# A three-block layer kernel: softmax in two steps, one 64-deep product in the delta rule's inversion, bias vectors made between the stages

## The chip, the cores and the metric

The kernel runs on one core of a Trainium2 chip. The metric is device time in microseconds (us) of one execution. Three runs of the kernel before gave 3664.62, 3666.99 and 3671.49 us; the median, 3666.99, is the time that the prediction starts from.

## The reference, cut to what matters

Three different blocks follow each other, on a sequence of 512 tokens (528 in the first, with 16 meta tokens ahead), width 1024:

```python
x = first_block(x, ...)    # RWKV-7 beside differential attention, then an MLP
x = second_block(x, ...)   # gated delta rule, GLA and HGRN2 mixers, then a grouped mixture of experts
x = third_block(x, ...)    # forgetting, block-sparse, stick-breaking and sliding-window attention
```

The change touches one piece of each. In block 1, the differential attention of 8 heads: each head has two softmaxes over the same keys, and its weights are their difference.

```python
s = jnp.where(pos[None, :] <= qpos[:, None], q @ k^T, neg)
pr = jax.nn.softmax(s, axis=-1)
attn_w = pr[:, :, 0] - lam * pr[:, :, 1]
o = attn_w @ v
```

In block 2, the gated delta rule of 4 heads, in chunks of 128 tokens, which solves a unit lower triangular system for each chunk:

```python
t_mat = a_strict + jnp.eye(c)
sol = lax.linalg.triangular_solve(t_mat, rhs, left_side=True, lower=True, unit_diagonal=True)
```

In block 3, two of the four kinds of attention (8 heads in all) add a bias that depends on the distance between query and key alone, looked up in a table of 32 buckets:

```python
s = s + rel_bias_h[:, rel_bucket(dist)]      # NEG_INF where dist < 0
```

## The kernel before

The program is one basic block for each engine, written by Python generators. `K.P`, `K.V`, `K.A` and `K.G` are TensorE (PE), VectorE (DVE), ScalarE (ACT) and GpSimd (POOL), and each records its instructions through helpers of one line each; these lines are the only ones that the profile can name: `tt` L361 (two tensors), `ts` L365 (scalars), `stt` L370, `cp` L373 (copy), `ms` L376 (memset), `rec` L379 (reciprocal), `red` L382, `scan` L385, `act` L346 and `copy` L354 on ScalarE, `mm` L425 and `tr` L429 (transpose) on PE. `did` or a last argument names an event that other engines wait for with `wait_ge(*at(...))`. `P.bank` takes a PSUM bank and waits until it was emptied. Weights stream from memory into a ring of five slabs ("ring"), are rounded by VectorE, ScalarE or POOL (`pool_half` does half a slab) and used by PE; everything else lies in one long SBUF tile ("arena").

The order on each engine is that of the generators. A `yield` ends a step; the next stream then gives its next step. Nothing is reordered: an engine that stands at a wait holds all that is behind it.

**Block 1, heads stage.** Eight pairs of RWKV heads are worked through, while a second stream, the differential attention, is advanced beside them at a pace of 0.7 (`Engine.advance`). In `dve_diff`, `scores(hd, i)` does VectorE's part of tile i of head hd: five query tiles a head (16 rows, then four times 128), their keys 16, 144, 272, 400 and 528 wide; 40 tiles in all. It waits for the scores in PSUM and takes two negated maxima. ScalarE then computes two exponentials with their sums. VectorE waits for each (`df_exp`), inverts the sums, scales the second matrix (`V.ts`) and combines both (`V.stt`). PE transposes these weights for the product with the values. `scores` has no yield of its own; the loop over tiles yields three times behind it (twice for i = 0).

**Block 2, mixers.** `both(delta, linear, 6, gates())` runs the delta rule's streams beside those of the other two mixers on each engine. The inversion of a 128-row triangle works on four chunks at a time, first with diagonal blocks of 32, doubled from 2 to 32 rows by the products Y, Z and ZT for l = 2, 4, 8, 16, then to 64 and 128. In the step Y 64, each chunk takes two products: one 64 rows deep with the second half of the leading triangle (`U.M0`, filled by ScalarE from `U.Xp` and from PE's `gd_m0`), one 32 rows deep with `U.Xp[32:64]`. At l = 2 to 16 VectorE also fills `U.M0` and `U.M1` with masks in turn.

**Block 2, experts' end.** After the last expert product `down(g)` the results go by VectorE and ScalarE copies into `m.ysb`, by DMA into `yd` in memory, and POOL gathers them back for each token into `m.yt` (`e_got`). VectorE adds the residual (L370) and takes the sums for the layer norm, ScalarE and VectorE normalize, and PE transposes (L429) into the layout of block 3.

**Block 3, start.** PE does the forget gate's projection, the first query projection and the root of the norm, then `rounds([dense(), local(), tables()])`: one step of each stream in turn. `dense` and `local` are the projections and attentions; `tables` makes the eight bias vectors. For vector i, VectorE first writes the column of bucket values, broadcast to 32 x 128, into `m.rb`; PE multiplies it with a one-hot matrix of buckets (a pass of high and low parts, so two PE instructions); VectorE copies the product into `m.vec[i % 2]`, whose rest it has set to -1e30; POOL (`pool_block3`) stores it into `skew[i]` in memory (the store is L3995) and loads it back with a row pitch one shorter (L4000), so that each row is shifted by one against the row above. That is `m.table[i]`, which PE adds to the scores of the later tiles. VectorE's rounds hold `forget()` beside these, the forget gate's chain: four ScalarE steps, then five on VectorE, the last a running sum, for which the scaling of the first query waits.

```python
def rounds(streams):
    while streams:
        for s in list(streams):
            try:
                next(s)
            except StopIteration:
                streams.remove(s)
```

Of the kernel before, what the change touches and what calls it, by code (L numbers as in the profile page):

```python
# [1619 lines left out]
def dve_diff(K, m):  # L1620
    V, at, ps, c, p, T, d, lam = K.V, K.book.at, K.ps, K.c, K.p, T1, m.df, m.lam

    def scores(hd, i):
# [25 lines left out]
    for hd in range(8):  # L1649
# [14 lines left out]
        for i in range(5):  # L1664
            scores(hd, i)
            yield
# [315 lines left out]
def memory2(K, x):  # L1982
# [12 lines left out]
    U.ATp, U.Xp, U.XTp, U.M0, U.M1, U.Yp = [M(128) for _ in range(6)]  # L1995
# [29 lines left out]
    m.yt = [m.xs[:, 1024 * j:1024 * j + 1024] for j in range(4)]  # L2025
# [53 lines left out]
def pe_mixers(K, m):  # L2079
# [81 lines left out]
    def delta():  # L2161
        for hd in range(4):
# [214 lines left out]
def act_mixers(K, m, bg):  # L2377
# [44 lines left out]
    def delta():  # L2422
        for hd in range(4):
# [185 lines left out]
def dve_mixers(K, m):  # L2609
# [47 lines left out]
    def delta():  # L2657
        for hd in range(4):
# [63 lines left out]
            for i, l in enumerate((2, 4, 8, 16)):  # L2722
# [8 lines left out]
                V.tt(U.XTp, U.XTp, bk("gd_xt", l, hd)[:, 0:128], ADD, "gd_xt", l, hd)  # L2731
                yield
# [275 lines left out]
def pe_experts(K, m):  # L3008
# [98 lines left out]
    for g in range(GROUPS):  # L3107
# [11 lines left out]
        down(g)  # L3119
    b = [P.bank(1, "normed", "ln2", k) for k in range(8)]  # L3120
# [9 lines left out]
def act_experts(K, m, yd):  # L3130
# [21 lines left out]
    for g in range(GROUPS):  # L3152
# [23 lines left out]
        for s in range(2):  # L3176
# [3 lines left out]
            A.eng.dma_start(yd[r0:r0 + 128, :], m.ysb[s]).then_inc(*K.book.up("yst%d" % s, ("e_st", g, s), by=16))  # L3180
    for j in range(4):
# [8 lines left out]
def dve_experts(K, m):  # L3190
# [27 lines left out]
    for g in range(GROUPS):  # L3218
# [26 lines left out]
        for kk in range(8):  # L3245
            dve_next(K, m.we, i)
            i += 1
        V.wait_ge(*at("slab", "experts", i - 1))
        if g:
            V.wait_ge(*at("e_st", g - 1, 1))  # L3250
        for h in range(2):
            V.cp(m.ysb[1][:, 512 * h:512 * h + 512], out_of(K, 1, T, "e_y", g, 2 + h), "e_y", g, 2 + h)
    for j in range(4):
# [168 lines left out]
def memory3(K, x):  # L3422
# [4 lines left out]
    m.vec, m.rb, m.table = [M(640) for _ in range(2)], M(128), [M(512 if i < 4 else 256) for i in range(8)]  # L3427
    m.d = []
# [36 lines left out]
                next(s)  # L3465
            except StopIteration:
                streams.remove(s)


def pe_block3(K, m):  # L3470
# [41 lines left out]
    def softmax_pair(t):  # L3512
# [4 lines left out]
        def scores(i):  # L3517
# [12 lines left out]
            else:  # L3530
                for r in range(2):
                    n, wide = (hd + r, 512) if kind == "moba" else (4 + hd + r, 256)
                    P.wait_ge(*at("table%d" % (n % 2), n))
# [97 lines left out]
    def tables():  # L3631
        for i in range(8):
            P.wait_ge(*at("tb_rb", i))
# [546 lines left out]
```

## Time and profile before

| | |
|---|---|
| median of three runs | 3666.99 us |
| the profiled execution, its time | 3679.07 us |
| its span in the trace | 3677.2 us |
| granted clock of PE, mean | 0.903 of full |
| busy: PE, DVE, ACT, POOL | 3218.3 (88%), 1663.1 (45%), 1220.4 (33%), 831.4 (23%) us |
| instructions on PE | 30118 |
| read from memory, written | 236.27 MB, 20.05 MB |

The profile was taken on an execution that ran 12 us longer than the median, so each duration below belongs to one of 3679 us. Busy shares are means over stages with different limits: the heads stage lies between 100 and 1126 us, the mixers between about 1780 and 2640, the experts end at 3126, block 3 begins at 3178. PE is the busiest engine everywhere; what an edit is worth depends on whether PE waits at its place, and for whom. A name such as "PE psum L425 <- DVE arena L361" reads: PE, before writing PSUM at line 425, waited for VectorE's operation of line 361 on the arena. In the timeline, what stands in square brackets is the idle time ahead of the instruction and what ended it.

### The profile page before, as it was taken

To read this page: it belongs to the slowest core of one execution; us is meant where nothing else is said; L and a number is where in the kernel's file an instruction comes from. 1 tells how busy PE (TensorE), PEld (TensorE's weight loads), DVE (VectorE), ACT (ScalarE), POOL (GpSimd) and SP (SyncE) were. 2 spreads that over 40 slices of the span, in tenths; PEclk is the share of its full clock that TensorE was granted. 3 is DMA by queue.
4 is the path that set the end of the run, shared out by engine and by line. 5 is a ranking of instruction groups with operands and counts; after the bars stand their busy time and mean duration, and the time that the engine had idled before them with its cause. 6 is when DMAs were issued, how large, how long until landed. Compare 5 with 4: busy or idle time off the path is not lost.

```text
span 3677.2 us, 70665 instructions
## 1 busy us (share of the span) xinstructions
PE 3218.3 (88%) x30118; PEld 2716.8 (74%) x30118; DVE 1663.1 (45%) x2925; ACT 1220.4 (33%) x2079; POOL 831.4 (23%) x808
## 2 busy tenths in 40 slices
PE   7888888898888999999889787887979999688887
PEld 6767777787777999999667666665769998345555
DVE  3544544444432434242343444556656665432342
ACT  2323323322322234232333334433344433232231
POOL 4122121121102200000245353543000002423232
PEclk9888888798877999999999898988999999778998
DMA  3001011010003332232122121213325555211111
GB/s 122 25 28 33 26 34 33 19 40 27 25 20 129 92 110 87 87 92 83 43 59 67 41 61 46 72 56 126 97 58 172 172 160 178 94 35 46 38 46 58
DMA packets 93962, 260.88 MB, mean 71 GB/s; under 512 B 10672, under 2 KB 10672, under 8 KB 92240
## 3 DMA queue, kind: packets, MB, share of 16 engines
q1 hardware_dynamic: 81072, 209.17, 19.2%
q0 software_dynamic: 7680, 35.66, 2.8%
q10 hardware_dynamic: 4896, 11.54, 0.8%
q8 instruction: 237, 3.88, 0.4%
q14 instruction: 77, 0.63, 0.1%
HBM read 236.27 MB, written 20.05 MB: 70 GB/s over the span
## 4 chain that ended last, share of the span: by engine, by line
PE 72%; DVE 13%; ACT 9%; issue 4%; DMA 2%; POOL 0%; DVEq 0%; ACTq 0%; SPq 0%; POOLq 0%
PE psum L425 70%; DVE arena L361 6%; ACT arena L346 5%; DVE arena L370 3%; ACT arena L354 2%; PE psum L429 1%; DMA ring<-in_w 1%; DVE arena L365 1%; ACT L342 1%; ACT L346 1%; DVE arena L382 1%; DVE arena L373 0%; DVE arena L388 0%; DVE arena L385 0%; DMA arena<-in_x 0%
## 5 line engine op out<-in xcount | busy, mean ns | idle before, releaser
L425 PE MATMUL psum<-arena,ring 128*128 128x264 f32 (+3 forms) x7720 | 1669.4, 340 | 24.5 <-DVE arena L361 11.8
L425 PEld LDWEIGHTS psum<-arena,ring 128*128 128x128 f32 (+1 forms) x7720 | 1269.5, 196 | 187.6 <-issue 43.5
L425 PE MATMUL psum<-arena 32*32 32x32 f32 (+19 forms) x16100 | 1027.2, 247 | 332.0 <-DVE arena L361 73.2
L425 PEld LDWEIGHTS psum<-arena 32*32 32x32 f32 (+13 forms) x16100 | 735.1, 138 | 589.6 <-issue 243.6
L425 PE MATMUL psum<-arena,arena 128*128 128x264 f32 (+2 forms) x5440 | 1005.4, 300 | 33.9 <-DVE arena L361 13.0
L425 PEld LDWEIGHTS psum<-arena,arena 128*128 128x128 f32 x5440 | 799.6, 188 | 86.7 <-issue 32.4
L354 ACT ACTIVATE arena<-psum 128x512 f32<-128x512 f32 (+14 forms) x656 | 299.9, 457 | 858.6 <-PE psum L425 703.2
L373 POOL CAST ring<-ring 128x512 fp32r<-128x512 f32 x332 | 221.2, 666 | 1320.8 <-DMA ring<-in_w 1312.1
L361 DVE TENSOR_TENSOR arena<-arena 128x528 f32<-128x528 f32 (+9 forms) x674 | 379.0, 562 | 238.0 <-ACT arena L346 126.9
L361 DVE TENSOR_TENSOR ring<-ring,arena 128x1024 fp32r<-128x1024 f32 (+1 forms) x250 | 293.6, 1174 | 349.4 <-ACT arena L354 346.8
L361 POOL TENSOR_TENSOR ring<-ring,ring 128x512 fp32r<-128x512 f32 x332 | 444.3, 1338 | 26.7
L346 ACT ACTIVATE arena<-arena 128x512 f32<-128x512 f32 (+8 forms) x494 | 292.5, 592 | 392.1 <-DVE arena L361 213.3
L354 ACT ACTIVATE arena<-ring 128x1024 fp32r<-128x1024 f32 (+1 forms) x250 | 254.9, 1020 | 481.3 <-PE psum L425 425.5
L361 DVE TENSOR_TENSOR arena<-arena,psum 88x192 f32<-88x192 f32 (+6 forms) x436 | 177.6, 407 | 406.6 <-PE psum L425 392.8
L370 DVE SCALAR_TENSOR_TENSOR arena<-arena 128x512 f32<-128x512 f32 (+8 forms) x237 | 178.6, 754 | 258.5 <-ACT arena L346 243.6
L346 ACT ACTIVATE arena<-psum,arena 128x528 f32<-128x528 f32 (+8 forms) x206 | 117.1, 568 | 292.4 <-DVE arena L382 180.8
L429 PE MATMUL psum<-arena 128*128 128x128 f32 (+2 forms) x693 | 114.9, 304 | 60.9 <-DVE arena L365 17.7
L429 PEld LDWEIGHTS psum<-arena 128*128 128x128 f32 (+2 forms) x693 | 86.3, 147 | 81.3 <-ACT arena L346 24.6
L361 DVE TENSOR_TENSOR arena<-psum,arena 88x264 f32<-88x264 f32 (+3 forms) x165 | 83.2, 504 | 119.1 <-PE psum L425 57.0
L370 DVE SCALAR_TENSOR_TENSOR arena<-psum,arena 128x528 f32<-128x528 f32 (+2 forms) x89 | 56.7, 638 | 160.8 <-PE psum L425 142.5
L382 DVE TENSOR_REDUCE arena<-psum 128x1 f32<-128x256 f32 (+8 forms) x128 | 57.1, 446 | 125.2 <-PE psum L425 122.2
L365 DVE TENSOR_SCALAR arena<-arena 128x512 f32<-128x512 f32 (+12 forms) x171 | 81.0, 474 | 72.2 <-ACT arena L354 48.8
(47 smaller groups left out, 885.3 us busy)
## 6 DMA issues: line engine op xcount, KB each, us to landing
ring<-in_w SPq DMA_DIRECT2D x202, 512.0 KB, 3.5
ring<-in_w SPq DMA_DIRECT2D x356, 256.0 KB, 2.6
bg<-arena ACTq DMA_DIRECT2D x24, 256.0 KB, 2.1
yd<-arena ACTq DMA_DIRECT2D x10, 512.0 KB, 5.0
arena<-in_x SPq DMA_DIRECT2D x2, 2112.0 KB, 11.3
arena<-bg POOLq DMA_DIRECT2D x1, 3072.0 KB, 18.1
od<-arena POOLq DMA_DIRECT2D x8, 264.0 KB, 3.7
oy<-arena POOLq DMA_DIRECT2D x8, 264.0 KB, 2.3
```

Source lines behind the costliest of these rows:

```text
L342: self.eng.preload_act_table_set("natural_log_exp_and_others")
L346: self.own(self.eng.activation(out, a, f, bias=bias, scale=scale, accum_out=accum), event)
L354: self.own(self.eng.activation(out, a, ACT.Copy, scale=scale), event)
L361: self.own(self.eng.tensor_tensor(out, a, b, op), event)
L365: self.own(self.eng.tensor_scalar(out, a, s1, None, op0), event)
L370: self.own(self.eng.scalar_tensor_tensor(out=out, in0=a, scalar=s, in1=b, op0=op0, op1=op1), event)
L373: self.own(self.eng.tensor_copy(out, a), event)
L382: self.own(self.eng.tensor_reduce(out, a, AXX, op, negate=neg), event)
L425: self.last_ins = self.eng.matmul(out, l, r, start=start, stop=stop, skip_group_check=skip)
L429: self.last_ins = self.eng.transpose(out, a, self.ident[0:n, 0:n])
```

## The change

Three edits, one in each block.

A. `scores` of `dve_diff` becomes a generator and yields once between the two maxima and the wait for the first exponential; one of the yields behind it goes, so that the number of steps stays.

B. The leading 64-row triangle of each chunk is kept in one place, `U.lead`, over the memory of `U.M0` and `U.M1`. Y 64 is one product for each chunk, 64 rows deep and 64 columns wide. ScalarE fills the two diagonal blocks from `U.Xp` (one copy more) and the block below the diagonal from `gd_m0`; VectorE zeroes the block above, behind its last addition for l = 16, and ScalarE's copy from `gd_m0` waits for that (`gd_lead`).

C. The eight bias vectors are made after the experts' last product. PE (`pe_tables`) reads the bucket values as a broadcast column, without `m.rb`; ScalarE copies the odd ones (`act_tables`), VectorE the even ones (`dve_tables`), each behind its last copy of the experts' results; VectorE sets the parts without a bias (`dve_no_tables`) before it waits for the last slab. `m.vec` is eight buffers, in memory that block 3 uses later for its heads (`m.d`), and `m.yt` moves elsewhere. POOL, at block 3's start, rounds four halves of slabs, issues all eight stores, then for each vector a half, the wait for its store, and the load. VectorE waits for all eight stores before its rounds, which have no `tables()` any more.

```diff
@@ dve_diff, scores @@
             V.red(sc[sub][:, 0:1], ps[0:qw, m0:m0 + W], MAX, "df_max", hd, i, sub, neg=True)
+        yield
         V.wait_ge(*at("df_exp", hd, i, 0))
...
         for i in range(5):
-            scores(hd, i)
-            yield
+            yield from scores(hd, i)
             if i:
                 yield
             yield
...
-    U.ATp, U.Xp, U.XTp, U.M0, U.M1, U.Yp = [M(128) for _ in range(6)]
+    U.ATp, U.Xp, U.XTp, U.Yp, U.M0, U.M1 = [M(128) for _ in range(6)]
+    U.lead = M.arena[:, M.top - 256:M.top].rearrange("p (j t) -> p j t", t=64)
...
             for j in range(4):
-                P.mm(bk(b)[64:128, 64 * j:64 * j + 32], U.AT[0:64, 128 * j + 64:128 * j + 128], U.M0[0:64, I4[j]])
-                P.mm(bk(b)[64:128, 64 * j + 32:64 * j + 64], U.AT[32:64, 128 * j + 64:128 * j + 128], U.Xp[32:64, I4[j]])
+                P.mm(bk(b)[64:128, 64 * j:64 * j + 64], U.AT[0:64, 128 * j + 64:128 * j + 128], U.lead[0:64, j, :])
             P.did("gd_inv", "Y", 64, hd)
...
             A.wait_ge(*at("gd_xt", 16, hd))
-            A.copy(U.M0[0:32], U.Xp[0:32])
+            A.copy(U.lead[0:32, :, 0:32], w4(U.Xp)[0:32])
             for q in range(4):
                 A.copy(v4(U.XT)[I4[q], :, I4[q]], w4(U.XTp)[I4[q]], *(("gd_diag", hd) if q == 3 else ()))
+            A.copy(U.lead[32:64, :, 32:64], w4(U.Xp)[32:64])
             yield
             A.wait_ge(*at("gd_inv", "Z", 32, hd))
-            A.copy(U.M0[32:64], bk("gd_m0", hd)[32:64, 0:128], "gd_m0", hd)
+            A.wait_ge(*at("gd_lead", hd))
+            A.copy(U.lead[32:64, :, 0:32], w4(bk("gd_m0", hd))[32:64], "gd_m0", hd)
...
                 V.tt(U.XTp, U.XTp, bk("gd_xt", l, hd)[:, 0:128], ADD, "gd_xt", l, hd)
+                if l == 16:
+                    V.ms(U.lead[0:32, :, 32:64], 0.0, "gd_lead", hd)
                 yield
...
         down(g)
+    pe_tables(K)
...
+        if g == GROUPS - 1:
+            dve_no_tables(K, m.third)
         V.wait_ge(*at("slab", "experts", i - 1))
...
+def pe_tables(K):
+
+    P = K.P
+    P.wait_ge(*K.book.at("con_oh"))
+    for i in range(8):
+        b = P.bank(1, "tb_v", i)
+        P.mm(K.ps[:, 512 * b:512 * b + 512], K.p["relb"][0:32, i:i + 1].to_broadcast([32, 128]), K.c["oh"][0:32])
+        P.did("tb_mm", i)
+
+
+def act_tables(K, m):
+    for i in range(1, 8, 2):
+        K.A.wait_ge(*K.book.at("tb_mm", i))
+        K.A.wait_ge(*K.book.at("tb_none"))
+        K.A.copy(*of_table(K, m, i), "tb_v", i)
+
+
+def dve_no_tables(K, m):
+    for i in range(8):
+        K.V.ms(m.vec[i][:, 512:640] if i < 4 else m.vec[i], -1e30, *(("tb_none",) if i == 7 else ()))
+
+
+def dve_tables(K, m):
+    for i in range(0, 8, 2):
+        K.V.wait_ge(*K.book.at("tb_mm", i))
+        K.V.cp(*of_table(K, m, i), "tb_v", i)
...
-            V.ts(m.rb[0:32], c["ones"][0:32], p["relb"][0:32, i:i + 1], None, MUL, None, "tb_rb", i)
...
-    rounds([dense(), local(), tables(), forget(), splits()])
+    for i in range(8):
+        V.wait_ge(*at("skewed%d" % i, i))
+    rounds([dense(), local(), forget(), splits()])
...
     G, eng = K.G, K.G.eng
-    for i, taken in enumerate(m.wz.after):
-        while m.wz.lows < taken + 3:
-            pool_half(K, m.wz)
-        W, n = (640, 512) if i < 4 else (384, 256)
+    for _ in range(4):
+        pool_half(K, m.wz)
+    for i in range(8):
+        W, skewed = m.vec[i].shape[1], "skewed%d" % i
         G.wait_ge(*K.book.at("tb_v", i))
-        eng.dma_start(skew[i][0:128 * W].rearrange("(p w) -> p w", w=W), m.vec[i % 2][:, 0:W]).then_inc(*K.book.up("skewed", ("skewed", i), by=16))
+        eng.dma_start(skew[i][0:128 * W].rearrange("(p w) -> p w", w=W), m.vec[i]).then_inc(*K.book.up(skewed, (skewed, i), by=16))
+    for i in range(8):
+        W, n, table = m.vec[i].shape[1], m.table[i].shape[1], "table%d" % i
         pool_half(K, m.wz)
-        G.wait_ge(*K.book.at("skewed", i))
+        G.wait_ge(*K.book.at("skewed%d" % i, i))
```

## Rows read from the trace of the kernel before

**Rows 1.** The page's chain of work that ended last, shares by engine.

```profile
PE 72%; DVE 13%; ACT 9%; issue 4%; DMA 2%; POOL 0%; DVEq 0%; ACTq 0%; SPq 0%; POOLq 0%
```

**Rows 2.** By stretch: length, PE, PEld, DVE, ACT, POOL busy, PEclk, DMA, GB/s.

```profile
100.00:1126.00 1026.00, 875.97 (x14804) 754.75 (x14804) 468.04 (x1070) 316.88 (x727) 171.81 (x180) 0.83 0.10 27
...
3178.40:3224.20 45.80, 37.48 (x107) 22.19 (x106) 18.33 (x36) 5.28 (x8) 23.45 (x31) 0.86 0.39 120
...
3226.00:3232.00 6.00, 6.00 (x27) 4.87 (x26) 1.44 (x2) 1.09 (x2) 3.76 (x4) 1.00 0.23 66
```

**Rows 3.** Waits from 100 to 1126 us: waiter, releaser: us, count, longest.

```profile
PE psum L425 <- DVE arena L361: 55.0, 32, 8.3
...
DVE arena L379 <- ACT arena L346: 32.2, 79, 1.8
```

**Rows 4.** Timeline of the heads stage: start, duration, instruction, [idle ahead, its releaser].

```profile
116.52 0.22 DVE L370 SCALAR_TENSOR_TENSOR arena<-arena 16x16 f32<-16x16 f32 x1
117.81 0.28 PE L425 MATMUL psum<-arena 64*88 64x88 f32 x1 [1.26 <-DVE arena L361]
...
581.68 0.16 DVE L379 RECIPROCAL arena<-arena 128x1 f32<-128x1 f32 x1 [0.66 <-ACT arena L346]
...
582.60 0.77 DVE L370 SCALAR_TENSOR_TENSOR arena<-arena 128x528 f32<-128x528 f32 x1
...
588.72 0.62 PE L425 MATMUL psum<-arena 88*64 88x64 f32 x5 [7.29 <-DVE arena L361]
...
592.96 1.23 PE L429 MATMUL psum<-arena 128*16 128x128 f32 x5
...
1108.75 0.48 PE L425 MATMUL psum<-arena 88*64 88x64 f32 x4 [2.39 <-DVE arena L361]
```

**Rows 5.** Groups by form, mixers (1780 to 2640 us): busy, mean ns, idle ahead.

```profile
L354 ACT ACTIVATE arena<-arena 32x128 f32<-32x128 f32 x20 | 6.1, 307 | 0.6
...
L425 PE MATMUL psum<-arena 32*64 32x32 f32 x32 | 5.7, 263 | 0.0
...
L425 PE MATMUL psum<-arena 64*64 64x32 f32 x32 | 5.6, 261 | 0.3 <-ACT arena L354 0.3
...
L425 PE MATMUL psum<-arena 64*64 64x64 f32 x32 | 3.9, 290 | 0.0
```

**Rows 6.** Timeline between the experts' end and block 3.

```profile
3125.76 1.42 DVE L373 COPY arena<-psum 128x512 f32<-128x512 f32 x2 [5.99 <-PE psum L425]
...
3136.06 1.53 DVE L370 SCALAR_TENSOR_TENSOR arena<-arena 128x1024 f32<-128x1024 f32 x1 [8.88 <-DMA arena<-yd,arena_whole]
...
3143.08 1.94 PE L429 MATMUL psum<-arena 128*128 128x128 f32 x8 [17.41 <-DVE arena L365]
...
3171.39 0.61 POOL L373 CAST ring<-ring 128x512 fp32r<-128x512 f32 x1 [21.30 <-DMA ring<-in_w]
```

**Rows 7.** Waits at block 3's start, 3178.4 to 3224.2 us.

```profile
PE psum L425 <- DVE arena L365: 8.3, 4, 4.9
```

**Rows 8.** Groups by form in the same stretch, PE.

```profile
L425 PE MATMUL psum<-arena,ring 128*128 128x512 f32 x89 | 28.6, 479 | 0.0
...
L425 PE MATMUL psum<-arena 32*128 32x512 f32 x16 | 9.6, 684 | 8.3 <-DVE arena L365 8.3
```

**Rows 9.** Timeline of the same stretch.

```profile
3179.22 2.80 ACT L346 ACTIVATE arena<-arena 4x512 f32<-4x512 f32 x4 [0.86 <-DVE arena L361]
...
3184.52 1.35 DVE L370 SCALAR_TENSOR_TENSOR arena<-arena 4x512 f32<-4x512 f32 x1
...
3190.20 1.79 PE L425 MATMUL psum<-arena 32*128 32x512 f32 x2 [4.93 <-DVE arena L365]
...
3203.52 0.38 DVE L376 MEMSET arena<- 128x384 f32 x1 [1.38 <-PE psum L425]
```

**Rows 10.** The stores of L3995: ns min/median/max, first and last start, time to landing.

```profile
L3995 POOL DMA_DIRECT2D skew<-arena x8: 544/544/609, 3182.7 to 3222.9; - x8
DMA to landing us min/median/max: 2.3/3.0/3.7
```

More of the change, by code:

```diff
@@ L2024, in memory2 @@
     m.xs_r, m.hot_r = M.rounded(m.xs, 512), M.rounded(m.hot, 256)
-    m.yt = [m.xs[:, 1024 * j:1024 * j + 1024] for j in range(4)]
+    m.yt = [M.arena[:, M.top - 5120 + 1024 * j:M.top - 4096 + 1024 * j] for j in range(4)]
     m.Hl = m.O[:, 4 * T:8 * T]
@@ L3180, in act_experts @@
             A.eng.dma_start(yd[r0:r0 + 128, :], m.ysb[s]).then_inc(*K.book.up("yst%d" % s, ("e_st", g, s), by=16))
+    act_tables(K, m.third)
     for j in range(4):
@@ L3252, in dve_experts @@
             V.cp(m.ysb[1][:, 512 * h:512 * h + 512], out_of(K, 1, T, "e_y", g, 2 + h), "e_y", g, 2 + h)
+    dve_tables(K, m.third)
     for j in range(4):
@@ L3426, in memory3 @@
     m.C4, m.Cn, m.Z4 = M(T), M(T), [M(T) for _ in range(3)]
-    m.vec, m.rb, m.table = [M(640) for _ in range(2)], M(128), [M(512 if i < 4 else 256) for i in range(8)]
-    m.d = []
+    m.table = [M(512 if i < 4 else 256) for i in range(8)]
+    m.d, m.vec, o = [], [], M.top
+    for i in range(8):
+        m.vec.append(M.arena[:, o:o + (640 if i < 4 else 384)])
+        o += 640 if i < 4 else 384
     for _ in range(2):
@@ L3532, in scores @@
                     n, wide = (hd + r, 512) if kind == "moba" else (4 + hd + r, 256)
-                    P.wait_ge(*at("table%d" % (n % 2), n))
+                    P.wait_ge(*at("table%d" % n, n))
                     P.mm(s_[r], c["ident"], m.table[n][:, wide - W:wide], False, True)
@@ L3629, in local @@
             off += 3 * SLAB
-    def tables():
-        for i in range(8):
-            P.wait_ge(*at("tb_rb", i))
-            b = P.bank(1, "tb_v", i)
-            P.wait_ge(*at("con_oh"))
-            P.mm(bk(b), m.rb[0:32, 0:128], c["oh"][0:32])
-            P.did("tb_mm", i)
-            m.wz.after.append(len(m.wz.offs))
-            yield
     b, bf, bq = P.bank(1, "root", "n3"), P.bank(1, "fx_forget"), P.bank(1, "fx_q", 0)
@@ L3657, in pe_block3 @@
         P.also("fx_proj", 0, "q")
-    rounds([dense(), local(), tables()])
+    rounds([dense(), local()])
     for k in range(8):
@@ L3937, in local @@
             yield from softmax_pair(t)
-    def tables():
-        for i in range(8):
-            v = m.vec[i % 2]
-            if i:
-                V.wait_ge(*at("tb_mm", i - 1))
-            V.ts(m.rb[0:32], c["ones"][0:32], p["relb"][0:32, i:i + 1], None, MUL, None, "tb_rb", i)
-            if i > 1:
-                V.wait_ge(*at("table%d" % (i % 2), i - 2))
-            if i < 4:
-                V.ms(v[:, 512:640], -1e30)
-                V.wait_ge(*at("tb_mm", i))
-                V.cp(v[:, 0:512], bk("tb_v", i), "tb_v", i)
-            else:
-                V.ms(v[:, 0:384], -1e30)
-                V.wait_ge(*at("tb_mm", i))
-                V.cp(v[:, 128:256], bk("tb_v", i)[:, 384:512], "tb_v", i)
-            yield
     def forget():
@@ L4039, in layout_engines @@
     K.mem.limit += at["con"]["sel16"][0] - early
-    m3 = memory3(K, m1.out)
+    m3 = m2.third = memory3(K, m1.out)
     od = nc.dram_tensor("od", [128, 8 * T1], F32, kind="Internal").ap()
```

5 lines of the change are left out of this document (4 added, 1 removed).

## The prediction, made before the change was run

> **What bounds the kernel now.** I read the page's chain of waits first: matmuls are 72% of the path that ends last, VectorE 13%, ScalarE 9% [rows 1]. So the question for each edit is which PE wait it shortens. Then the table by stage [rows 2]: in the first block's head stage (100 to 1126 us) PE is busy 876 of 1026 us, so 150 us are PE waits; in the 45.8 us of block 3 in which the bias tables are made, 37.5, of which much is the tables themselves. Then who waits for whom in the head stage [rows 3]: VectorE stands still 32.2 us, in 79 stops, for the exponentials whose sums it inverts, and PE waits 55.0 us for VectorE products of L361. Last the order of time around three places [rows 4, 6, 9].
>
> **Part A, the softmax in two steps (40 tiles).** Before, VectorE takes two maxima, then stops for ScalarE's two exponentials, then does two reciprocals, a product, a scaling and a weighted sum. After, the maxima end the step, and the rest comes at the stream's next turn, behind a piece of RWKV work. Nothing is added or removed, 32.2 us of stops [rows 3] can vanish, and the arithmetic behind them moves. Its size: for the widest tile from the second reciprocal at 581.68 to the end of the sum at 583.37, and the first reciprocal (0.16), 1.85 us; in the narrowest the sum takes 0.22 in place of 0.77 us [rows 4], the scaling falls by half as much, so 1.0 us; the widths between are evenly spaced, so 1.4 us a tile, 57 us for 40.
> How much lies on the path? At 588.72 PE had waited 7.29 us for VectorE, which had worked without a gap since the tile: its arithmetic (1.85) and its second stop (0.66) alone were 2.5 us of that wait [rows 4]. I went through all PE waits of over 0.9 us for VectorE in this stage and found 14 with a softmax tile directly ahead, the first at 117.81 (1.26 us) and the last at 1108.75 (2.39 us) [rows 4]. Of each I took the smaller of the wait and the tile's part: 31.6 us in all, the upper bound. That is 31.6 / (32.2 + 57) = 35% of what the tiles put between maxima and next work. The arithmetic doesn't vanish: at its new place it should meet a waiting PE as often as at the old, so it costs 0.35 x 57 = 20 us there, and the gain is the stops' share, 0.35 x 32.2 = **11 us**. Bounds: 31.6 us if the new places are all free, and a loss of up to 57 us if all of them are on the path and the old ones weren't; I stay at the middle, since old and new places are of the same kind. The weights get later by one turn; PE transposed them at 592.96, 9.6 us after they were ready [rows 4], so I cost that at nothing. Were that margin gone, each microsecond of it would be PE's.
>
> **Part B, one product for two in the delta rule's inversion (4 heads).** The two forms of the step, 64 rows and 32 rows deep, keep PE busy 5.6 and 5.7 us; the 64x64 form, also 32 instructions, 3.9 us [rows 5]. The new product is of that form: 11.3 - 3.9 = 7.4 us less PE time. Added: one ScalarE copy of a 32x128 block a head at 0.31 us, 1.2 us in all [rows 5], in the queue ahead of the copy for which this very product waits, and a VectorE memset of 32x128, behind the addition that PE wants. The trace has no such memset here; nothing and the tables' 128x384 one, 0.38 us [rows 9], bound it, and I take 0.2 us, as a third of the columns is nearer to the lower end; VectorE's next turn bears it. ScalarE's new wait on the memset holds the copy that PE wants and behind it the other stream's work; the memset is issued long before. Two streams share PE here, and while one waits the other fills, so I count half of 7.4 - 1.2: **3 us**, bounds 7.4 and a loss of 2.
> The page "TensorE: Matmul & The Clock Gate" of the Trainium skill, section "LDWEIGHTS (loading the stationary operand)", has a weight load cost its columns / 1.2 ns whatever its depth. That the 32-row form is as dear as the 64-row one agrees. By its figure, 53 ns for 64 columns, 32 loads less would give an estimate of 1.7 us of PE time, and this term would be 1 us.
>
> **Part C, the bias vectors made between the stages.**
> Removed from block 3: eight pairs of PE instructions (16, busy 9.6 us), and PE's waits for the broadcast column that VectorE made for each, 8.3 us [rows 7, 8]; also eight VectorE scalings, eight memsets and eight copies. What is left to PE between 3178.4 and 3224.2 is 89 projection matmuls and one column sum. At the full clock 27 such matmuls took 6.00 us [rows 2], so 89 take 19.8, with the sum of 1.1 us (a pair, as dear as a table's) 20.9. What is late next: the forget gate's chain. ScalarE's four steps end at 3182.02 (3179.22 + 2.80), VectorE's five (from 3184.52 on before, end 3190.1, less 0.3 for the column made among them) take 5.3 us [rows 9], so the first query tile is scaled at about 3187.4 and its square reaches PE at 3189; by then PE has run out of the five pieces (30 matmuls, 6.7 us) that the other stream offers, and waits some 2.9 us. Start-up about 1 us. So 20.9 + 2.9 + 1 = 24.8 against 45.8: 21 us; a clock that falls during that wait takes one back: **20 us**. Bounds: 45.8 - 20.9 = 25, and 13 if only the 9.6 and less than half of the 8.3 come back. Behind 3224 PE is busy throughout in both, and the tables are wanted only by later tiles, so this carries to the end. Could the ring of weights starve PE? It fed the 27 matmuls in 6.00 us without a gap [rows 2], so I cost it at nothing.
> Added between the stages: eight pairs on PE at 1.2 us (9.6 us), or 1.79 at the lower clock (14 us) [rows 8, 9], in an idle stretch of 17.41 us before 3143.08 [rows 6]. VectorE's four copies follow their products, the last the seventh. With 1.2 us from 3125.8 on it ends at about 3134.6, before the gathered rows arrive at 3136.06 [rows 6]: cost nothing. With 1.79 it ends at 3138.7, and the normalization behind it is late by 2.6 us: that is the price if this cover is gone. The eight memsets, 0.38 us each at most [rows 9], 3 us, lie in the 5.99 us that VectorE waits for the last expert product [rows 6]; ScalarE's four copies end before the rows arrive, too, and it has no part in the normalization before VectorE's first sums.
> DMAs: POOL issues the eight stores in one row, at some 0.55 us each [rows 10], behind four weight halves. Before, it had done five halves 21.30 us ahead of 3171.39 [rows 6], so the stores are out at 3155 at the latest, and the last has landed 3.7 us later at most [rows 10], 3158. VectorE waits for it before block 3's streams, and comes there at 3179 [rows 9]; 21 us of cover. Behind the stores on POOL stand the fifth weight half, for PE's work after 3179, and the table loads.
> The page "SBUF — State Buffer" of the Trainium skill, section "A bandwidth-pool intuition that's wrong (but worth ruling out)", has a POOL DMA of 620 ns take 3100 while a VectorE copy holds the shared port. The rows show 544 to 609 ns for all eight stores [rows 10], beside short VectorE work. Now they would fall beside 1024-wide sums. By the page they would end 20 us later, at 3178: just not the last, and a reason to give that rival a chance at all.
>
> **Sum.** 11 + 3 + 20 = 34 us. The profiled run took 3679.07 us (span 3677.2), 12 us above the median of 3666.99; 3679 - 34 = 3645 for it, and for the median **3633 us**, -0.9%.
>
> **Rivals.** (1) The stall only moves: VectorE comes to the next turn with the exponentials done but the arithmetic hits PE there, A gives 0: 3667 - 23 = 3644 us. For it: the turn follows the state updates, on which PE waits. (2) A gives all of its 31.6 us, and PE, less idle, keeps the clock that is 0.83 of full in this stage [rows 2]: 3667 - 23 - 32 - 3 = 3609 us. For it: the widest tile's new place lies behind the update chain. (3) The gain of C is taken back, since the ring of weights or the store wait ends last instead: C gives nothing, A and B do, 3653 us; with A at 0 too 3664 us. Against: 21 us of cover. (4) Slower: in the head stage the moved arithmetic lands between the product that PE is waiting for and its release, while the old places were free. Its price is up to 57 us; with C and B whole, it makes the kernel slower once over 23 / 57 = 40% of the moved time is newly on the path; all of it gives 3667 + 57 - 23 = 3701 us, 60% gives 3678. Against: 35% is on the path at the old places already.
>
> **How the numbers follow.** Forecast 3633, own range 3622 to 3641 (0.48); rival 1, 3644 (0.22); rival 2, 3609 (0.14); rival 3, 3653 to 3664 (0.10); rival 4 (0.06). The 8-in-10 range runs from rival 2's to past rival 1's and into rival 3's, 3609 to 3655. A measurement of this kernel can tell 0.2% (7 us) from no change: faster by more 0.87, within 0.07, slower 0.06.
>
> **What would show it.** Right: the reciprocals' 32.2 us of stops nearly gone and PE's 55.0 us behind L361 lower by 10 to 20; PE in the head stage done 10 us sooner; the first key sum 21 us nearer the forget gate; gathered rows still the last thing before the normalization; no VectorE wait on the stores. Wrong: a new PE wait behind L370 or L361 of the same size; VectorE stopped before block 3's streams; the transposes at the lower clock starting late.

## The result, and the profile after

The changed kernel takes 3620.09 us (median of four runs, 3616.27 to 3625.63), the kernel before 3668.89 us with one more run (3664.62 to 3671.49). The ratio is 0.9869 with a 95% interval of 0.9852 to 0.9887: 48 us less (41 to 54), where the forecast was 34 less and the range reached from 12 to 58 less. The sign and the range hold; the size is 14 us short.

The page of the changed kernel, its span, the busy times and the chain by engine, beside the table of before and [rows 1]:

```profile
span 3614.5 us, 70601 instructions
...
PE 3188.3 (88%) x30086; PEld 2691.1 (74%) x30086; DVE 1656.2 (46%) x2917; ACT 1223.4 (34%) x2087; POOL 830.0 (23%) x808
...
PE 73%; DVE 12%; ACT 9%; issue 4%; DMA 2%; POOL 0%; ACTq 0%; DVEq 0%; SPq 0%; POOLq 0%
```

PE has 32 instructions less, 30 us less busy time, and the same share. The products that part B merges are 8.6 of these 30 us (below); the others are the same instructions, shorter on the whole, at a mean granted clock of 0.912 instead of 0.903. The other half of the gain was PE's waiting. The windows of the changed kernel that hold the same work as the stages of before: the heads stage (the same instructions as the first of [rows 2], 14804 there), the mixers, and block 3 from the forget gate's first product to the first key sum. The columns are those of [rows 2].

```profile
100.00:1094.00 994.00, 857.83 (x14805) 739.95 (x14805) 467.33 (x1071) 317.33 (x728) 171.03 (x180) 0.86 0.10 28
...
1744.00:2591.00 847.00, 699.80 (x4843) 548.45 (x4843) 440.60 (x677) 320.53 (x500) 356.69 (x322) 0.91 0.22 67
...
3132.20:3159.70 27.50, 23.46 (x92) 17.96 (x90) 9.01 (x12) 5.29 (x8) 17.20 (x20) 0.94 0.39 115
```

The heads stage went from 1026 to 994 us, and block 3's start from 46.2 (3178.4 to 3224.6 before) to 27.5 us. The mixers' same stretch of before, 1780 to 2636, was 856 us, so 9 less. These are 32, 9 and 18.7 us between two executions, of which the one before was 10 us above its median. How much of that is the execution shows in the heads stage of three of the experiments below (part B alone, part C alone, and the inversion's step fourfold), whose instructions are those of before there:

```profile
100.00:1122.00 1022.00, 869.02 (x14805) 749.15 (x14806) 470.26 (x1071) 317.90 (x729) 171.82 (x181) 0.84 0.10 28
...
100.00:1120.00 1020.00, 865.36 (x14804) 746.15 (x14804) 465.97 (x1070) 317.07 (x727) 172.07 (x180) 0.84 0.10 28
```

```profile
100.00:1114.00 1014.00, 865.50 (x14792) 746.57 (x14792) 465.06 (x1067) 314.96 (x724) 171.64 (x180) 0.84 0.10 28
```

The same stage took 1022, 1020 and 1014 us there, with a granted clock of 0.84 against 0.83. The mixers of part C alone, whose instructions there are those of before too:

```profile
1774.10:2622.00 847.90, 707.19 (x4876) 553.99 (x4875) 441.63 (x673) 319.38 (x496) 357.01 (x322) 0.91 0.22 67
```

That is 8 us less than the 856 with nothing changed, so the pair of traces says nothing of part B. One trace is good to some 10 us in these two stages. Block 3's start is steadier: from the forget gate's first product to the first key sum, ten traces of kernels that leave it as before took 45.7 to 47.4 us, and three with all of part C 27.5 to 28.3. What follows uses times of several runs, and traces for where it happened.

### The profile page after: what moved, and what is told of

Read it like the earlier page. It is cut to its first block, busy times and chain, and to the rows that moved or that the text cites. A ratio compares the mean times of both kernels' runs of the same rounds, so it can differ in the third digit from the quotient of the medians.

```text
span 3614.5 us, 70601 instructions
## 1 busy us (share of the span) xinstructions
PE 3188.3 (88%) x30086; PEld 2691.1 (74%) x30086; DVE 1656.2 (46%) x2917; ACT 1223.4 (34%) x2087; POOL 830.0 (23%) x808
## 4 chain that ended last, share of the span: by engine, by line
PE 73%; DVE 12%; ACT 9%; issue 4%; DMA 2%; POOL 0%; ACTq 0%; DVEq 0%; SPq 0%; POOLq 0%
PE psum L425 71%; DVE arena L361 6%; ACT arena L346 5%; ACT arena L354 3%; DVE arena L370 3%; PE psum L429 2%; ACT L342 1%; DMA ring<-in_w 1%; DVE arena L365 1%; ACT L346 1%; DVE arena L382 1%; DVE arena L373 0%; DVE arena L388 0%; DMA arena<-in_x 0%; DVE arena L385 0%
## 5 line engine op out<-in xcount | busy, mean ns | idle before, releaser
L425 PE MATMUL psum<-arena,ring 128*128 128x264 f32 (+3 forms) x7720 | 1654.8, 338 | 26.4 <-DVE arena L361 11.3
L425 PE MATMUL psum<-arena 32*32 32x32 f32 (+18 forms) x16068 | 1010.1, 245 | 310.4 <-ACT arena L346 71.9
L425 PEld LDWEIGHTS psum<-arena 32*32 32x32 f32 (+12 forms) x16068 | 720.5, 136 | 568.2 <-issue 239.5
L361 DVE TENSOR_TENSOR arena<-arena 128x528 f32<-128x528 f32 (+8 forms) x674 | 378.6, 562 | 243.2 <-ACT arena L346 125.8
L361 DVE TENSOR_TENSOR ring<-ring,arena 128x1024 fp32r<-128x1024 f32 (+1 forms) x250 | 293.6, 1174 | 346.1 <-ACT arena L354 343.5
L361 POOL TENSOR_TENSOR ring<-ring,ring 128x512 fp32r<-128x512 f32 x332 | 443.5, 1336 | 26.7
L354 ACT ACTIVATE arena<-ring 128x1024 fp32r<-128x1024 f32 (+1 forms) x250 | 254.9, 1020 | 478.4 <-PE psum L425 426.0
L361 DVE TENSOR_TENSOR arena<-arena,psum 88x192 f32<-88x192 f32 (+6 forms) x436 | 177.6, 407 | 402.3 <-PE psum L425 388.4
L370 DVE SCALAR_TENSOR_TENSOR arena<-arena 128x512 f32<-128x512 f32 (+8 forms) x237 | 178.1, 751 | 253.8 <-ACT arena L346 247.1
L361 DVE TENSOR_TENSOR arena<-psum,arena 88x264 f32<-88x264 f32 (+3 forms) x165 | 83.2, 504 | 118.4 <-PE psum L425 57.9
L370 DVE SCALAR_TENSOR_TENSOR arena<-psum,arena 128x528 f32<-128x528 f32 (+2 forms) x89 | 56.7, 638 | 169.2 <-PE psum L425 150.9
L3366 POOL DMA_INDIRECT ring<-in_w,arena_whole x24 | 24.4, 1015 | 390.4 <-PE psum L425 390.4
```

What stands on the lines that cost most here:

```text
L354: self.own(self.eng.activation(out, a, ACT.Copy, scale=scale), event)
L361: self.own(self.eng.tensor_tensor(out, a, b, op), event)
L370: self.own(self.eng.scalar_tensor_tensor(out=out, in0=a, scalar=s, in1=b, op0=op0, op1=op1), event)
L425: self.last_ins = self.eng.matmul(out, l, r, start=start, stop=stop, skip_group_check=skip)
L3366: G.eng.indirect_dma_start(K.ring[:, slot * SLAB:slot * SLAB + SLAB], None, by_row, bass.IndirectOffsetOnAxis(ap=m.place[:, 4:5], axis=0), ...
```

## The experiments

All are changes of the kernel before unless said otherwise, and each was timed beside it on the same chip. "us less" is the ratio's distance from one, times the median of before of that group (3673.61, 3671.98 and 3671.13 us), with the interval of the ratio behind it.

### The three parts alone, and the whole again

The edits are those of the three parts of the diff above. What was expected of part A alone:

> Part A alone. The change as a whole gave 49 us by the medians where 34 was the forecast, and the two traces drift apart by 35.8 us up to the end of the heads stage. Theory 1 (the forecast's: only the stops' share leaves the path, the arithmetic meets a waiting PE at its new place as often as at the old): 11 us less than the kernel before. Theory 2 (the new place is nearly free, so the arithmetic leaves the path too): 25 to 32 us less. If the 35.8 us are partly a difference between two executions, theory 1 stays possible; this run decides it.

Part B alone:

> Part B alone. Theory 1 (the forecast's): 3 us less, since the other stream hides half of the 7.4 us of PE time and the added copy and memset take some back. Theory 2 (the inversion is the longest chain of the mixers and PE's saving counts whole): 7 to 9 us less, as the 9.3 us by which the two traces drift apart in the mixers suggest.

Part C alone:

> Part C alone. Theory 1 (the forecast's): 20 us less than before, all of it between 3178 and 3224 us, none given back between the stages. Rival (part of it is given back in block 3, as the traces' distance falls from 64.9 to 60.5 us there): 14 to 16 us less.

The whole:

> The whole change again, on the chip of the three parts. If the parts don't touch each other, its gain is the sum of theirs, within 3 us, and near 49 us. If PE's clock or a shared engine ties them together, it is not.

| kernel | median, us | ratio, interval | us less |
|---|---|---|---|
| part A | 3650.57 | 0.9939, 0.9917 to 0.9962 | 22 (14 to 30) |
| part B | 3666.38 | 0.9982, 0.9964 to 1.0000 | 7 (0 to 13) |
| part C | 3652.79 | 0.9949, 0.9933 to 0.9966 | 19 (12 to 25) |
| whole | 3619.48 | 0.9855, 0.9823 to 0.9887 | 53 (42 to 65) |

22 + 7 + 19 = 48 us, against 53 (42 to 65) for the whole beside them and 48 in the first comparison: within these intervals the parts add up. C came as forecast (20), B is nearer to 7 than to 3 though its interval holds both, and A is twice its 11 us. The question is A.

### A: the arithmetic moved alone, the stops kept

```diff
         V.rec(sc[1][:, 2:3], sc[1][:, 1:2])
+        yield
         V.tt(sc[1][:, 2:3], sc[1][:, 2:3], lam[0:qw, 4:5], MUL)
...
-            scores(hd, i)
-            yield
+            yield from scores(hd, i)
```

> Only the arithmetic moves: VectorE still stops for both exponentials and takes both reciprocals right behind the maxima, then yields, and the product, the scaling and the weighted sum (1.2 us a tile, some 50 us for 40) come at the next turn. Theory 1 (the forecast's, old and new places are alike): same time as the kernel before, since the stops stay and the arithmetic costs the same at both. Theory 2 (the new place is nearly free; part A alone gave 23 us): about half of part A's gain, 10 to 14 us less. With the stops kept the gain can't be theirs.

3652.62 us, ratio 0.9956 (0.9939 to 0.9974): 16 us less (10 to 22). The two rows of waits that matter, from 100 to 1090 us, first of this kernel, then of part A alone (before, [rows 3]):

```profile
PE psum L425 <- DVE arena L361: 47.4, 32, 7.0
...
DVE arena L379 <- ACT arena L346: 31.8, 79, 1.8
```

```profile
PE psum L425 <- DVE arena L361: 38.6, 28, 5.8
...
DVE arena L379 <- ACT arena L346: 5.3, 13, 0.6
```

VectorE still stands 31.8 us at the reciprocals, and yet most of the gain is there. The reciprocals stay at the old place here; the product, the scaling and the sum move. The forecast's statement that old and new places are alike falls: a gain without any stop taken away can only come from what the moved arithmetic delays.

### A: what a microsecond of VectorE costs at each place

```diff
         V.ts(Pt[1], Pt[1], sc[1][:, 2:3], None, MUL, None)
+        for _ in range(4):
+            V.ts(Pt[1], Pt[1], 1.0, None, MUL, None)
```

In the kernel before:

> The price of VectorE time at the old place: the kernel before with four more scalings by one of the second matrix in each tile (4 x 0.53 us for the widest, 4 x 0.30 us for the second narrowest, some 58 us of VectorE in all; the numbers computed don't change). Both theories: 0.35 of it lies on the path, so 20 us more than the kernel before. If it costs under 10 us the share of 35% was read too high from the 14 waits, over 30 us and it was too low, and A's gain needs no free new place.

The same lines in part A:

> The price of VectorE time at the new place: part A with the same four scalings more in each tile, 58 us of VectorE. To be compared with part A alone (23 us less than before). Theory 1 (places alike): 20 us more than part A, so 3 us less than the kernel before. Theory 2 (new place nearly free): under 8 us more than part A, so 15 us or more less than before.

At the old place 3708.13 us, ratio 1.0109 (1.0077 to 1.0142): 40 us more (28 to 52). At the new place 3664.07 us, ratio 0.9992 (0.9973 to 1.0012): 3 us less than before (10 less to 4 more), so 19 more than part A (9 to 30). The group of scalings (L365) that holds those of the softmax tells the work added (heads stage of before, then padded at the old place):

```profile
L365 DVE TENSOR_SCALAR arena<-arena 128x528 f32<-128x528 f32 (+4 forms) x47 | 19.4, 413 | 1.7
```

```profile
L365 DVE TENSOR_SCALAR arena<-arena 16x16 f32<-16x16 f32 (+4 forms) x207 | 70.0, 338 | 7.2
```

160 instructions more and 50.6 us, not the 58 that I had put down. So a microsecond cost 40 / 50.6 = 0.8 us at the old place and, with 48.8 us added (67.9 against 19.1 in part A), 19 / 48.8 = 0.4 at the new one.

### A: the arithmetic taken away at each place

```diff
-        V.tt(sc[1][:, 2:3], sc[1][:, 2:3], lam[0:qw, 4:5], MUL)
-        V.ts(Pt[1], Pt[1], sc[1][:, 2:3], None, MUL, None)
-        V.stt(Pt[0], Pt[0], sc[0][:, 2:3], Pt[1], MUL, ADD, "df_w", hd, i)
+        V.tt(sc[1][:, 2:3], sc[1][:, 2:3], lam[0:qw, 4:5], MUL, "df_w", hd, i)
```

> What the arithmetic costs at the old place, measured by taking it away: the kernel before without the scaling of the second matrix and without the weighted sum in all 40 tiles (some 37 us of VectorE; the weights are then the first exponentials, not normalized, so this part of the computation is left out). The 58 us added at the old place cost 36 to 40 us. Theory 1 (a straight price: 0.65 a microsecond both ways): 24 us less than before. Theory 2 (a bent price: taking away saves only what PE waits now, 35% by the forecast's 14 waits, adding costs more since each wait starts at once): 10 to 16 us less.

The same edit in part A:

> The same two instructions left out at the new place (part A without the scaling and the weighted sum). To be compared with part A alone, 23 us less than before. Theory 1 (a straight price at the new place too, 0.3 a microsecond by the padded run): 11 us less than part A. Theory 2 (bent): 0 to 5 us less than part A, the arithmetic at its new place costs next to nothing. The difference of this run and the one without arithmetic at the old place is what the stops alone are worth: the forecast said 11 us, parts A and the moved arithmetic alone (23 and 16 to 19) say 4 to 7.

At the old place 3648.87 us, ratio 0.9937 (0.9923 to 0.9951): 23 us less (18 to 28). At the new place 3639.55 us, ratio 0.9906 (0.9889 to 0.9923): 34 us less (28 to 41), 12 less than part A. The 12 have an interval of 2 to 22. In the heads stage the groups of L365 and L370 went from 19.4 us and 60.7 us (92 of them) to these in the first kernel. (Both leave the scaling and the sum out, so their weights are not normalized.)

```profile
L370 DVE SCALAR_TENSOR_TENSOR arena<-arena 128x528 f32<-128x528 f32 x51 | 38.8, 760 | 44.8 <-ACT arena L346 43.4
...
L365 DVE TENSOR_SCALAR arena<-arena 128x528 f32<-128x528 f32 x7 | 3.7, 528 | 0.2
```

That is 15.7 + 21.9 = 37.6 us of work taken away (one of the 41 sums lies behind the window's edge, 0.8 us), so 23 / 37.6 = 0.6 for each at the old place; at the new one 35.3 us and 12, 0.3. Adding and taking away give about the same price: 0.6 to 0.8 at the old place, 0.3 to 0.4 at the new one. Each of the four has a wide interval, but the padded and the emptied kernel of one place can be set against each other without the kernel between them: at the old place (40 + 23) / (50.6 + 37.6) = 0.71 (0.57 to 0.86), at the new one (34 - 3) / (48.8 + 35.3) = 0.37 (0.25 to 0.49). The places differ by 0.34 (0.15 to 0.53). The bent price of theory 2 is not needed.

The difference of the two emptied kernels, 34 - 23 = 11 us (3 to 19, with both intervals), is what the stops are worth together with what was still moved: the 80 reciprocals, 12.9 us, and the small products, some 8 us. At 0.34 a microsecond these 21 us make 7, so some 4 are left to the stops. Part A less the arithmetic alone says 22 - 16 = 6, with the reciprocals moved in it (4 us), so 2. The intervals are wider than these numbers.

### A: one turn later still

```diff
+        yield
+        yield
         V.wait_ge(*at("df_exp", hd, i, 0))
```

(with one yield less behind `scores`.)

> The rest of the softmax two turns behind the maxima in place of one (the number of steps stays). Theory 1: as part A, 23 us less, since all stops are gone with one turn already and every place costs the same. Theory 2: it depends on what stands at the second place; if the weights' margin ahead of the transposes (9.6 us in one case) is used up, PE waits at the transposes and the gain falls to 0 to 15 us.

3646.43 us, ratio 0.9932 (0.9906 to 0.9959): 25 us less (15 to 35), as part A within the intervals. One turn is enough, and a second costs nothing that the times show.

### B: the step's products issued four times

```diff
-            for j in range(4):
+            for j in 4 * list(range(4)):
                 P.mm(bk(b)[64:128, 64 * j:64 * j + 32], U.AT[0:64, 128 * j + 64:128 * j + 128], U.M0[0:64, I4[j]])
```

> The price of PE time in the inversion's step Y 64: the kernel before with each of its products issued four times in place of once (the same values into the same place), 3 x 11.3 = 34 us of PE more over the four heads. Theory 1 (the forecast's: the other stream fills half): 17 us more than before. Theory 2 (the inversion's chain is the longest, every microsecond counts, part B gave 7 us): 34 us more. Under 8 us: the other stream hides nearly all, and part B's gain is not PE's time in this step.

3700.06 us, ratio 1.0080 (1.0066 to 1.0094): 29 us more (24 to 35). The two forms in its mixers, against 5.6 and 5.7 us in [rows 5]:

```profile
L425 PE MATMUL psum<-arena 64*64 64x32 f32 x128 | 24.7, 282 | 0.3 <-ACT arena L354 0.3
...
L425 PE MATMUL psum<-arena 32*64 32x32 f32 x128 | 24.7, 281 | 0.0
```

49.4 - 11.3 = 38.1 us of PE cost 29: 0.77 of it (0.64 to 0.91), not the half that I counted. The second stream covers little of this step.

### C: the broadcast column alone

```diff
-            P.wait_ge(*at("tb_rb", i))
-            P.mm(bk(b), m.rb[0:32, 0:128], c["oh"][0:32])
+            P.mm(bk(b), K.p["relb"][0:32, i:i + 1].to_broadcast([32, 128]), c["oh"][0:32])
```

(and without `V.ts(m.rb ...)` and VectorE's wait for the product before it.)

> One piece of part C alone: the tables stay in block 3, but PE reads the bucket values as a broadcast column, so VectorE's eight scalings and PE's waits for them (8.3 us) go. Theory 1 (the forecast's reading: of the 8.3 us, 2.9 are the forget gate's chain and stay): 5 us less than before; the rest of part C's 19 us is then the products' own 9.6 us and their start-up. Rival (the waits were all of the column): 8 us less. If it gives 0, the products and the forget chain carry all of part C's gain.

3666.67 us, ratio 0.9990 (0.9973 to 1.0006): 4 us less (10 less to 2 more), which can't be told from nothing, nor from theory 1's 5 or the rival's 8. The trace shows more. Its forget gate's first product is at 3164.41 and the first key sum here:

```profile
3164.41 0.68 DVE L361 TENSOR_TENSOR arena<-psum,arena 4x512 f32<-4x512 f32 x1 [10.32 <-ACT arena L346]
...
3203.93 2.05 PE L425 MATMUL psum<-arena 128*128 128x512 f32 x2 [2.34 <-ACT arena L346]
```

So 39.5 us lie between them against 46.2 before (3178.45 to 3224.64) and 27.5 after. The column is worth 6.7 of the 18.7 us in this stretch; 12 go with the products themselves and what follows them. The stretch itself, then all that is behind it to the end, and the same end of before:

```profile
3164.40:3203.90 39.50, 34.72 (x108) 20.19 (x107) 15.84 (x28) 5.28 (x8) 23.59 (x32) 0.91 0.47 142
3203.93:3663.60 459.67, 394.18 (x1596) 261.42 (x1596) 151.14 (x342) 139.45 (x301) 126.09 (x131) 0.85 0.15 43
```

```profile
3224.64:3677.20 452.56, 382.99 (x1597) 256.06 (x1595) 150.94 (x342) 139.34 (x301) 125.96 (x131) 0.87 0.15 43
```

Against [rows 2] PE's busy time in the stretch fell by 2.8 us for the same work, at a granted clock of 0.91 in place of 0.86, so not all of the 6.7 us were waits. And the 6.7 us are gone at the end of this execution: what is behind takes 7.1 us more, with PE busy 11 us longer for the same matmuls, at a clock of 0.85 against 0.87. Ten traces with that part as before took 452.3 to 456.0 us for it. Whether the column causes this is open, one trace can't tell; but the gain of the stretch is no gain of the kernel that was shown.

## Why the prediction was right or wrong, step by step

**Part A's mechanism, right in some tiles.** The tile that the prediction took apart, [rows 4] at 581.68, in the changed kernel (the same columns):

```profile
566.47 0.71 DVE L370 SCALAR_TENSOR_TENSOR arena<-arena 128x528 f32<-128x528 f32 x1
567.21 0.36 DVE L379 RECIPROCAL arena<-arena 128x1 f32<-128x1 f32 x2
...
567.80 0.49 DVE L365 TENSOR_SCALAR arena<-arena 128x528 f32<-128x528 f32 x1
568.33 0.77 DVE L370 SCALAR_TENSOR_TENSOR arena<-arena 128x528 f32<-128x528 f32 x1
569.13 2.19 DVE L361 TENSOR_TENSOR arena<-arena 128x528 f32<-128x528 f32 x3
571.36 0.47 DVE L361 TENSOR_TENSOR arena<-arena,psum 88x64 f32<-88x64 f32 x2
571.64 4.30 PE L425 MATMUL psum<-arena 88*64 88x64 f32 x26 [5.83 <-DVE arena L361]
```

Before, the first of its reciprocals had stopped too:

```profile
580.86 0.16 DVE L379 RECIPROCAL arena<-arena 128x1 f32<-128x1 f32 x1 [0.80 <-ACT arena L346]
```

Now both run back to back, without a stop. The scaling and the sum still stand ahead of the same L361 work for which PE waits: 5.83 in place of 7.29 us. The 1.46 us gained are the two stops (0.80 and 0.66), and the arithmetic of this tile costs at the new place what it cost at the old. This is the forecast as written.

**Part A's mechanism, wrong in others.** The first tile, where PE had waited 1.26 us at 117.81 [rows 4]:

```profile
115.46 0.36 DVE L382 TENSOR_REDUCE arena<-psum 16x1 f32<-16x16 f32 x2 [0.42 <-PE psum L425]
116.57 1.82 DVE L361 TENSOR_TENSOR arena<-psum,arena 88x264 f32<-88x264 f32 x4 [0.75 <-PE psum L425]
118.42 0.34 DVE L379 RECIPROCAL arena<-arena 16x1 f32<-16x1 f32 x2
```

VectorE now goes from the maxima to the L361 work that PE wants, and does the softmax behind it; PE has no wait at that place. Stops and arithmetic are both gone from it. What is left is smaller: PE's transpose of these weights waits 0.41 us for the sum (L370), a wait that was not there before. Over the stage, PE's waits for L361 fell as forecast, by 10 to 20 us, from the 55.0 of [rows 3]; in the changed kernel, from 100 to 1090 us:

```profile
PE psum L425 <- DVE arena L361: 40.7, 27, 5.8
```

**The steps of A that failed** are two. The first is "it should meet a waiting PE as often as at the old, ... since old and new places are of the same kind". A microsecond costs 0.71 us (0.57 to 0.86) at the old places and 0.37 (0.25 to 0.49) at the new ones. The prediction put this difference at nothing; over the 57 us moved it is 19 us (9 to 30), and the kernel that moves only the product, the scaling and the sum, some 45 us, gained 16 (10 to 22). The reason was in the prediction as rival 2's ("the widest tile's new place lies behind the update chain"), though for the widest tile looked at above it isn't true. The second is the share of 35%. It was read from 14 waits of over 0.9 us with a tile directly ahead; the price at the old place is about twice that. Nor was 31.6 us an upper bound: at 0.71 the 57 us alone cost 40 us (32 to 49) at the old places. What stands of A is the sign and that the stops go; their own worth, forecast at 11, comes out at some 2 to 4, with intervals that reach past 11. With the 19 us for the places that makes 21 to 23 of the 22 measured (14 to 30).

Where does the price come from that the waits don't show? The heads stage of the old place padded, and of the old place without the arithmetic:

```profile
100.00:1166.00 1066.00, 884.29 (x14804) 762.50 (x14804) 519.82 (x1231) 316.81 (x727) 172.05 (x180) 0.82 0.09 26
```

```profile
100.00:1088.00 988.00, 849.70 (x14791) 734.41 (x14792) 427.52 (x988) 315.38 (x724) 172.08 (x180) 0.86 0.10 29
```

PE's idle time (length less busy) is 182 us in the first, 138 in the second, and 149 to 155 in the four kernels with the stage as before. Its busy time for the same matmuls also moves: 884 and 850 us against 865 to 876, with a granted clock of 0.82 and 0.86. The four take 1020.5 us on average, 869 of them busy; so of the 45 us more of the padded stage some 15 are longer matmuls at the lower clock, and a count of waits leaves them out. PE's waits for VectorE, for all its lines, rose from 86 to 115 us there. The four differ by 11 us in busy time, and the padded execution ran 9 us above its kernel's median, the emptied one 7 below, so the size of this part is rough. Nor does PE's idle time alone set it. Part A alone, then padded:

```profile
100.00:1097.00 997.00, 863.77 (x14794) 745.43 (x14796) 465.46 (x1068) 314.99 (x724) 170.90 (x180) 0.85 0.10 28
```

```profile
100.00:1109.00 1009.00, 858.50 (x14804) 738.40 (x14804) 514.43 (x1229) 316.32 (x726) 172.29 (x180) 0.86 0.10 28
```

Here idle time rose from 133 to 151 us and busy time fell by 5. What sets the clock in this stage stays open.

**Part B.** The term was mis-sized in its last factor. PE's saving was 7.4 forecast; the 64x64 form of part B alone holds both steps now, 6.6 us for 64 instructions:

```profile
L425 PE MATMUL psum<-arena 64*64 64x64 f32 x64 | 6.6, 258 | 1.0 <-issue 0.8 <-ACT arena L354 0.2
...
L354 ACT ACTIVATE arena<-arena 32x128 f32<-32x128 f32 x24 | 7.4, 307 | 0.8
...
L376 DVE MEMSET arena<- 32x128 f32 x4 | 0.7, 165 | 0.3
```

That is 5.6 + 5.7 + 3.9 - 6.6 = 8.6 us saved. The copy (four more of 0.31 us) and the memset (0.165 us, 0.2 forecast) cost what was put down. "While one waits the other fills, so I count half" is the step that failed: 0.77 x (8.6 - 1.3) = 5.6, within the measured 7 (0 to 13). The traces say more when all are taken. Two marks that each of them has, a product at the mixers' start and a copy of a slab at their end, in the kernel before:

```profile
1795.16 5.12 PE L425 MATMUL psum<-arena,ring 128*40 128x512 f32 x16 [4.89 <-DVE arena L370]
...
2636.18 1.07 ACT L354 ACTIVATE arena<-ring 128x1024 fp32r<-128x1024 f32 x1 [11.14 <-PE psum L425]
```

Between them lie 841.0 us here, 832.7 to 845.6 in the ten executions with the step as before (840 on average), and 829.6 to 831.7 in the three with part B: 9 us less (6 to 12). That is near PE's whole saving, not half of it.

The estimate by the page "TensorE: Matmul & The Clock Gate" of the Trainium skill, section "LDWEIGHTS (loading the stationary operand)", made this term 1 us (less the 1.2 us of the copy and halved, as the term itself was, its 1.7 us would be 0.3). By its 53 ns for 64 columns the 192 instructions more of the kernel with the step fourfold would be 10 us of PE; they were 38.1 us, nearly 200 ns each. The load alone is no price for an instruction of this size here.

**Part C.** Right in size and nearly all its steps. The stretch gave 18.7 us in the traces and 19 (12 to 25) in the times against 20. PE's wait for the forget gate was forecast at 2.9 us and is 3.81:

```profile
3142.89 1.10 PE L425 MATMUL psum<-arena 128*128 128x512 f32 x2 [3.81 <-ACT arena L346]
...
3159.74 1.10 PE L425 MATMUL psum<-arena 128*128 128x512 f32 x2 [0.27 <-ACT arena L346]
```

The clock was the other term too small. PE was busy 23.46 us in the stretch, forecast 20.9 and 1 for the clock. During that wait and just behind it (the window with 0.09 us of PE is the wait):

```profile
3139.00:3142.90 3.90, 0.09 (x2) 0.05 (x1) 3.57 (x6) 0.63 (x1) 3.22 (x5) 1.00 0.34 96
3142.90:3145.00 2.10, 2.10 (x6) 1.42 (x7) 0.00 (x0) 0.89 (x2) 2.01 (x3) 0.82 0.24 62
3145.00:3150.00 5.00, 5.00 (x17) 3.95 (x17) 0.75 (x1) 0.43 (x1) 1.93 (x4) 0.74 0.26 79
```

The granted clock was 1.00 through the wait and fell behind it, to 0.82 and 0.74.

The work put between the stages cost nothing, as said. The timeline there:

```profile
3079.88 11.17 PE L425 MATMUL psum<-arena 32*128 32x512 f32 x16
3080.04 2.14 DVE L373 COPY arena<-psum 128x512 f32<-128x512 f32 x3 [2.86 <-issue]
...
3089.45 0.29 DVE L373 COPY arena<-psum 128x128 f32<-128x128 f32 x1 [3.12 <-PE psum L425]
...
3090.33 1.57 DVE L370 SCALAR_TENSOR_TENSOR arena<-arena 128x1024 f32<-128x1024 f32 x1 [0.59 <-DMA arena<-yd,arena_whole]
```

PE's eight pairs take 11.2 us in all, between the forecast's 9.6 and 14. The normalization starts 10.29 us after VectorE's first copy of the last results, 10.30 before ([rows 6]: 3125.76 to 3136.06), and is still released by the gathered rows. But VectorE's last vector copy ends only 0.59 us ahead of it: that is what is left of the 8.88 us of cover. Behind the first key sum the three kernels with part C take 453.9 to 454.8 us to their ends, ten with block 3 as before 452.3 to 456.0, so no loss is shown there.

The stores, for which VectorE waits, and their landing:

```profile
L4015 POOL DMA_DIRECT2D skew<-arena x8: 539/539/609, 3101.8 to 3105.6; - x8
...
DMA to landing us min/median/max: 2.5/3.7/3.8
```

The last has landed by 3110, and VectorE starts on block 3 at 3132.24: 22 us of cover, 21 forecast. The rule of the page "SBUF — State Buffer" of the Trainium skill, section "A bandwidth-pool intuition that's wrong (but worth ruling out)", did not show: the stores took 539 to 609 ns each, not some 3100. But the page's 3100 ns are for a DMA beside a VectorE copy, and the prediction applied them to sums. No copy fell beside the stores; until 3104.29 VectorE ran these, then only short work and nothing from 3104.72 on:

```profile
3101.61 1.23 DVE L370 SCALAR_TENSOR_TENSOR arena<-arena 128x1024 f32<-128x1024 f32 x1
3102.87 1.42 DVE L3266 BATCH_NORM_STATS2 arena<-arena 128x6 f32<-128x512 f32 x2
```

So these sums didn't hold up a store, and what a copy would do no run here shows.

**The rivals.** Rival 1 (A gives nothing) and rival 3 (C is taken back) are refuted by the parts alone. Rival 2 had the right direction for A, but 22 (14 to 30) of its 32 us. Rival 4 needed the new places to be dearer than the old; they cost half. The time, 3620, lies between the likeliest case and rival 2, two microseconds under the likeliest case's own range.

## What to carry to other kernels

A wait taken out of a shared in-order queue also moves the work behind it, and where that lands can be worth more than the wait: price each place by adding a known amount of work there and by taking it away. Waits counted with a threshold and a neighbour gave half the price here. That a second stream shares an engine is no reason to count half: this inversion paid about 0.8 of each microsecond. And a gain read in one stretch must be followed to the kernel's end: the broadcast column's 6.7 us didn't arrive there.

## What the runs showed that was not expected

PE's busy time for some 14800 instructions of the heads stage went from 850 to 884 us with nothing changed on PE, at granted clocks of 0.86 and 0.82. PE's idle time, 138 and 182 us, goes with it in these two, but not in part A and its padded kernel. Kernels with identical instructions in the stage took 1014 to 1026 us for it, so a change of that size is not to be read off two traces; block 3's start, some 46 us long, repeated within 1.7 us over ten.
